# Paired 512-column matmuls in the feed-forwards, roots pair by pair in the first mixture, the difference attention's norm as work in front

## The reference, cut to what matters

```python
# first mixture (gated linear attention), per head of 128 values
o = gla_chunked(q, k, v, log_g)
o = o * rsqrt(mean(square(o), -1) + 1e-5) * head_g
o = from_heads(o) * silu(r)
out = concat([o, memory_attention(qm, mem)]) @ w_out
...
# second block, two layers
h = rms_norm(x, ffn1_norm); x = x + 0.5 * (silu(h @ w_gate) * (h @ w_up)) @ w_down   # 1024 -> 2816 -> 1024
h = rms_norm(x, mix_norm)
o_a = neighborhood_attention(...)        # 4 heads  ("na")
o_b = diff_attention(...)                # 4 heads of two softmaxes, then rms_norm per head  ("df")
o_c = gqa_axial_attention(...)           # 4 heads  ("gq")
o_d = dilated_attention(...)             # 4 heads  ("dl")
x = x + concat([o_a, o_b, o_c, o_d]) @ w_out
h = rms_norm(x, ffn2_norm); x = x + 0.5 * (silu(h @ w_gate) * (h @ w_up)) @ w_down
```

## Time and profile before

| | |
|---|---|
| median of 3 runs | 3088.6 us (3087.66 to 3089.96) |
| the profiled execution's own time | 3092.74 us |
| its span | 3090.5 us |
| busy in the span: PE, DVE, ACT, POOL | 3000.8 us (97%), 2109.8 us (68%), 1628.2 us (53%), 469.1 us (15%) |
| chain that ended last | PE 89%, DVE 6%, ACT 3%, issue 1% |
| mean granted TensorE clock | 0.983 of full speed |
| DMA | 509.47 MB, 165 GB/s |

### The profile page before, as it was taken

The page is one execution under the profiler, slowest core; times in us unless marked ns, Lnnn a source line. Parts: engine busy times, 40 slices in busy tenths (PEclk is TensorE's granted clock), DMA queues, the critical chain, the costliest instruction groups (busy, mean ns, idle before and its releaser), DMA issues.

```text
span 3090.5 us, 56441 instructions
## 1 busy us (share of the span) xinstructions
PE 3000.8 (97%) x21828; PEld 2712.4 (88%) x21828; DVE 2109.8 (68%) x4512; ACT 1628.2 (53%) x3157; POOL 469.1 (15%) x363
## 2 busy tenths in 40 slices
PE   8989999999999989999999999899989999998999
PEld 8789999988887879999998888799868999987898
DVE  4559978799755555997879965655765565566555
ACT  5445544454555555554444455555655555565554
POOL 1212200000022112220000012123101222311122
PEclk9999999999999999999999999999999999999999
DMA  6345554454555335554454555465423556542354
GB/s 216 121 144 182 181 175 161 158 170 164 191 191 177 127 100 174 178 186 163 160 166 163 167 198 191 153 219 185 152 75 132 189 176 214 185 162 76 130 184 157
DMA packets 138363, 509.47 MB, mean 165 GB/s; under 512 B 15329, under 2 KB 15858, under 8 KB 136818
## 3 DMA queue, kind: packets, MB, share of 16 engines
q1 hardware_dynamic: 134352, 489.22, 48.0%
q10 hardware_dynamic: 3746, 16.65, 1.5%
HBM read 504.76 MB, written 1.05 MB: 164 GB/s over the span
## 4 chain that ended last, share of the span: by engine, by line
PE 89%; DVE 6%; ACT 3%; issue 1%; DMA 0%; POOL 0%; ACTq 0%; DVEq 0%
PE ps L475 88%; PE ps L479 1%; ACT WH L1152 1%; DVE WL L1758 1%; ACT BIG L1291 1%; DVE XTl L1830 0%; DVE BIG L1994 0%; DVE BIG L1799 0%; DVE BIG L2500 0%; DVE BIG L1847 0%; DMA BIG<-in_memT 0%; DVE BIG L1989 0%; DVE BIG L2451 0%; DVE H L1924 0%; DVE BIG L1855 0%
## 5 line engine op out<-in xcount | busy, mean ns | idle before, releaser
L1152 ACT ACTIVATE WH<-RAW 128x512 fp32r<-128x512 f32 x1866 | 1158.4, 630 | 1082.1 <-PE ps L475 1068.7
L1758 DVE TENSOR_TENSOR WL<-RAW,WH 128x512 fp32r<-128x512 f32 x1537 | 1102.7, 725 | 710.1 <-ACT WH L1152 698.8
L475 PE MATMUL ps<-XTh,WH 128*128 128x256 f32 x3928 | 1128.4, 287 | 19.8 <-DVE XTl L1807 8.7
L475 PE MATMUL ps<-XTl,WH 128*128 128x256 f32 x3928 | 1118.4, 285 | 0.0
L475 PE MATMUL ps<-XTh,WL 128*128 128x256 f32 x3928 | 1118.0, 285 | 0.0
L2562 POOL TENSOR_TENSOR WL<-RAW,WH 128x512 fp32r<-128x512 f32 x329 | 440.5, 1339 | 2593.6 <-ACT WH L1152 2593.6
L475 PEld LDWEIGHTS ps<-XTh,WH 128*128 128x128 f32 x3928 | 760.2, 194 | 28.6 <-issue 9.8
L475 PEld LDWEIGHTS ps<-XTl,WH 128*128 128x128 f32 x3928 | 760.8, 194 | 2.9
L475 PEld LDWEIGHTS ps<-XTh,WL 128*128 128x128 f32 x3928 | 760.2, 194 | 0.0
L475 PE MATMUL ps<-WH,GH 128*128 128x512 f32 x1056 | 420.2, 398 | 6.5 <-DVE BIG L2435 2.0
L475 PE MATMUL ps<-WH,GL 128*128 128x512 f32 x1056 | 413.7, 392 | 0.0
(11 more groups left out here) (197 smaller groups left out, 2590.7 us busy)
## 6 DMA issues: line engine op xcount, KB each, us to landing
RAW<-in_w SPq DMA_DIRECT2D x933, 512.0 KB, 3.3
BIG<-in_ln ACTq DMA_DIRECT2D x4, 1024.0 KB, 7.8
BIG<-in_sk ACTq DMA_DIRECT2D x2, 1024.0 KB, 5.1
BIG<-in_na_bias ACTq DMA_DIRECT2D x2, 1024.0 KB, 5.0
BIG<-in_qk_gain ACTq DMA_DIRECT2D x2, 960.0 KB, 5.8
BIG<-in_memT ACTq DMA_DIRECT2D x4, 256.0 KB, 7.6
BIG<-in_xT ACTq DMA_DIRECT2D x1, 1024.0 KB, 5.3
H<-in_x ACTq DMA_DIRECT2D x1, 1024.0 KB, 8.1
```

The source lines that it names most:

```text
L475: return self.e.matmul(out, lhsT, rhs, start=start, stop=stop, skip_group_check=loose)
L1152: e.activation(wh, raw, ACT.Copy).then_inc(*c.hi.mark(j))
L1758: e.tensor_tensor(wl, raw, wh.bitcast(F32), ALU.subtract).then_inc(*c.lo_v.mark(j))
```

## The change

1. **Feed-forwards.** `XTh` and `XTl` become two halves of one tensor `XT`, so that each chunk's 512 columns lie side by side. From group 2 on, gate and up have a bank each (6 and 7 for even f, 4 and 5 for odd), and `wide_cols` does, per half of the weights, four matmuls of 512 columns (high weights with both parts of the tokens) and four of 256 (low weights with the high part). The two halves of the bank must then be added: ScalarE copies columns 256 to 512 of both banks (`PARTS`), and VectorE adds them.
2. **The difference attention's norm.** `od` is taken out of `bg`, and is put in `fg` by `attend` as soon as df is complete. `until` waits for `"od"` ahead of chunk 2 of the output product. `until` now prefers `bg`, except for `"od"`.
3. **First mixture.** The decays are multiplied pair by pair; sum, logarithm, exponential, Newton step and gated product are made for each pair of heads (`gla_root`, `gated_heads`) as soon as it is there. The last part of `vr` is evicted with Silu, for which a tiny Silu loads the table beforehand.
4. **Evictions.** `halves(n, done)` on ScalarE waits for `used` and evicts ahead of the last half's other work and split (GLA, SBM, queries of PEER).
5. **First depth product.** `depth` with `first` waits for each bank where it is first written, and does the second block of tokens first.

```diff
@@ Pace
     def until(self, name):
         while name not in self.reached:
-            q = self.fg or self.bg
+            q = self.bg if self.bg and name[1] != "od" else self.fg or self.bg
@@ Chip
+        self.XT = sb("XT", [P, 8, 512], FR)
+        self.XTh, self.XTl = self.XT[:, :, 0:256], self.XT[:, :, 256:512]
+    def ffn_banks(self, f):
+        if f < 2:
+            return self.B[4 + f][:, 0:256], self.B[4 + f][:, 256:512]
+        return (self.B[6], self.B[7]) if f % 2 == 0 else (self.B[4], self.B[5])
@@ Tensor
+    def wide_cols(self, key, ps):
+        c = self.c
+        for half in range(2):
+            j, wh, wl = self.half(key)
+            parts = blocks(4)
+            for a in range(4):
+                self.mm(ps[:, :], wh[:, parts[a]], c.XT[:, half * 4 + a, :], half + a == 0, half * 4 + a == 7, loose=True)
+            for a in range(4):
+                t = self.mm(ps[:, 0:256], wl[:, parts[a]], c.XTh[:, half * 4 + a, :], False, half * 4 + a == 7, loose=True)
+            t.then_inc(*c.used.mark(j))
+            self.pace.tick()
     def depth(self, key, ah, al, first):
-            for blk in range(2):
-                t = self.three(c.B[blk * 2 + half][:, :], ah[:, TB[blk]], al[:, TB[blk]], wh, wl, first, False)
+            for blk in (1, 0) if first else (0, 1):
+                out = c.B[blk * 2 + half]
+                if first:
+                    out = self.bank(blk * 2 + half)
+                t = self.three(out[:, :], ah[:, TB[blk]], al[:, TB[blk]], wh, wl, first, False)
     def inner(self):
-            e.wait_ge(*c.vec.at("ke"))
+            e.wait_ge(*c.vec.at("qe", p))
     def ffn_stage(self, layer, which):
-            ps = self.bank(4 + f % 4)
-            self.cols(("fg", layer, which, f), ps[:, 0:256], stage if f == 0 else None)
-            self.cols(("fu", layer, which, f), ps[:, 256:512])
-            self.empty[4 + f % 4] = c.vec.at(stage, "hid", f)
+            if f < 2:
+                ...
+            else:
+                for b, key in zip((6, 7) if f % 2 == 0 else (4, 5), ("fg", "fu")):
+                    self.wide_cols((key, layer, which, f), self.bank(b))
+                    self.empty[b] = c.vec.at(stage, "hid", f)
     def attend(self, stage, name, k):
+        if name == "df":
+            self.pace.fg.append(od_steps(self.pace, stage))
     def mix_stage(self, layer):
-        pace.bg.insert(2, od_steps())
-                         lambda ch: pace.until((stage, NAMES[ch // 2])))
+                         lambda ch: pace.until((stage, "od" if ch == 2 else NAMES[ch // 2])))
@@ Scalar
-    def halves(self, n):
-        for _ in range(n):
+    def halves(self, n, done=None):
+        for k in range(n):
             self.j += 1
+            if done and k == n - 1:
+                self.e.wait_ge(*self.c.used.at(self.j - 1))
+                done()
             self.pace.tick()
             self.split()
     def states(self):
+            if p:
+                self.gla_root(p - 1)
+            if p == 2:
+                e.activation(t.rs[:, 63:64], c.ONE, ACT.Silu).then_inc(*c.act.mark())
     def gla_stage(self):
-            self.halves(8)
-            e.wait_ge(*c.used.at(self.j - 1))
-            for blk in range(2):
-                e.activation(t.vr[...], c.B[2 * (r % 2) + blk][:, :], ACT.Copy)
+            def done():
+                for blk in range(2):
+                    e.activation(t.vr[...], c.B[2 * (r % 2) + blk][:, :], ACT.Silu if r == 2 else ACT.Copy)
+            self.halves(8, done)
-        e.wait_ge(*c.vec.at("sum", 2))
-        self.rsqrt(t.rs[:, 0:12], ..., "rsum")
-        e.activation(t.vr[:, :, 1024:1536], t.vr[:, :, 1024:1536], ACT.Silu).then_inc(*c.act.mark("silu", 1))
         e.preload_act_table_set(TABLES)
+        self.gla_root(2)
     def hidden(f):   # feed-forward
+            if f >= 2:
+                for k, ps in enumerate(c.ffn_banks(f)):
+                    e.wait_ge(*c.used.at(BASE[stage] + 4 * f + 2 * (f - 2) + 1 + 2 * k))
+                    if f >= 4:
+                        e.wait_ge(*c.vec.at(stage, "hid", f - 2))
+                    e.activation(t.PARTS[:, 2 * r + k, :], ps[:, 256:512], ACT.Copy).then_inc(*c.act.mark(stage, "parts", f, k))
@@ Vector
     def inner(self):
-        e.tensor_tensor(t.qT, t.qT, t.EB, ALU.mult).then_inc(*c.vec.mark())
-        e.tensor_tensor(t.EN, t.EN, t.kT, ALU.mult).then_inc(*c.vec.mark())
+        for p in range(3):
+            e.tensor_tensor(t.qT[:, p], t.qT[:, p], t.EB[:, p], ALU.mult).then_inc(*c.vec.mark())
+            e.tensor_tensor(t.EN[:, p], t.EN[:, p], t.kT[:, p], ALU.mult).then_inc(*c.vec.mark("qe", p))
     def states(self):
+            if p == 2:
+                self.gla_root(0)
+                self.gated_heads(0)
     def hidden(f):   # feed-forward
+            else:
+                e.wait_ge(*c.act.at(stage, "parts", f, 0))
+                e.tensor_tensor(t.GR[:, r, :], gate[:, 0:256], t.PARTS[:, 2 * r, :], ALU.add).then_inc(*c.vec.mark())
+                self.own()
+                e.tensor_tensor(t.GR[:, r, :], t.GR[:, r, :], c.RB, ALU.mult).then_inc(*c.vec.mark(stage, "gr", f))
+                e.wait_ge(*c.act.at(stage, "parts", f, 1))
+                e.tensor_tensor(t.UP[:, r, :], up[:, 0:256], t.PARTS[:, 2 * r + 1, :], ALU.add).then_inc(*c.vec.mark("up", stage, f))
+                up = t.UP[:, r, :]
+                self.own()
```

125 lines of the change are left out of this document (68 added, 57 removed).

## The result

The changed kernel takes 3068.3 us (median of 6 runs, 3063.28 to 3073.09), the one before beside it 3088.1 us (3087.41 to 3089.96): a ratio of 0.9935, interval 0.9922 to 0.9948. A second set of the same kernel gave 3071.2 us (3064.48 to 3072.72) and the same ratio, 0.9935 [0.9921, 0.9949]. It is faster by about 20 us; 30.6 were forecast. The profiled execution took 3072.22 us with a span of 3070.3 and a mean granted clock of 0.987.

A forecast was written before the change was run, and what follows sets the result against it. TensorE's own list was taken to bound PEER and feed-forwards, and waits for other engines the joints and mixtures. Savings of 15.4 + 9.0 + 3.6 + 2.6 = 30.6 us from 3088.6 gave 3058 us, range 3046 to 3073.

The forecast's parts named there:

- the high end: Top of the forecast range, 3073 us: mixture waits only move (3067), plus lower bounds of chain (2.4) and other evictions (2.6).
- The low end: Bottom of the forecast range, 3046 us, said to take the mixtures at their upper bound.
- The pace: Feed-forwards: one matmul fewer per chunk saves 13.3 ns, 360.0 to 346.7 ns; 1280 chunks give 17.0 us less.
- 512-column starts further apart than 0.23 us: Feed-forwards: a trace sign, listed in advance, that would show the prediction wrong.
- the remainder is not per matmul: Feed-forwards: rival that a chunk keeps its 360 ns, giving 0 in place of 17.0 us, 3075 us; chance 0.06.
- The Trainium skill's rule: Feed-forwards: gap of columns over 2.4 GHz plus 2.5 ns; about 3 us saved instead of 17, total 3072 us.
- The tail: End of each feed-forward stage: the longer chain costs 0.4 us per stage, 1.6 us for four.
- The chain of `hidden`: Feed-forwards: chain grows 0.48 us from 3.57, free inside a stage with 1.4 us left.
- Mixtures: Second block's mixtures: 3.9 us wait becomes 2.3, clock returns 2.5, banks 0.4; 4.5 us each, 9.0 for both.
- Stage 0: First mixture: 1.9 us wait, 1.5 clock and 0.5 eviction saved, 0.3 new waiting; 3.6 us less.
- The decays pair by pair I cost at nothing: First mixture: pairwise decays cost nothing, since TensorE is in a half while VectorE makes them.
- Other evictions: PEER copies one split earlier save 1.1 us, the stick-breaking wait for the last bank 1.5; together 2.6 us.

The follow-up runs named there:

- last_narrow: product_later with the last block (21) of each feed-forward in the old narrow form, in one bank; 3064.2 us, ratio 0.9921.
- product_later: silu_later plus, on VectorE, pair 0's root and product behind the sum of pair 2, and pairs 1 and 2's behind the preceding low copies; 3063.9 us, ratio 0.9921.
- silu_later: The changed kernel with the first mixture's small table-loading Silu moved on ScalarE behind the high copy of pair 3; 3064.4 us, ratio 0.9918.
- root0_early: product_later with pair 0's root and product back ahead of the sum of pair 2; 3066.8 us, ratio 0.9928.
- undo_stage0: The changed kernel with the first mixture's pairwise roots, products, decays and merged Silu put back as before, early evictions kept; 3074.8 us, ratio 0.9950.
- both_fixes: root0_early and last_narrow together; 3066.6 us, ratio 0.9926.
- undo_ffn: The changed kernel with its feed-forwards put back: one bank per block, three 256-column matmuls a chunk; 3075.1 us, ratio 0.9957.
- undo_norm: The changed kernel with the difference attention's norm back in the background queue and the old order of `until`; 3077.2 us, ratio 0.9963.
- undo_evict: The changed kernel with evictions behind their half's split again and four banks waited for at once; 3069.3 us, ratio 0.9934.
- alternate: The changed kernel with wide and narrow feed-forward matmuls in turn, one of each, instead of four and four; 3071.4 us, ratio 0.9940.
- long_bursts: The changed kernel with eight wide then eight narrow feed-forward matmuls, both halves of the weights held; 3106.4 us, ratio 1.0050.

## Why the prediction was right, and where not

The time lies in the range and on the forecast side, at 20 of the forecast 30.6 us. That it lies in the range is in part luck: the high end was made of mixtures that give nothing and of lower bounds of the chain and the evictions, none of which came, while the two things that cost most, the pace and stage 0, had no such room. The low end is added up wrongly: the mixtures at their upper bound give 3058 - 8.8 = 3049 us, and 3046 only with the best bounds of the other terms as well. By its steps:

**The pace.** "A chunk costs ... 226.7 + 120.0 = 346.7 ns" is the step that was mis-sized. Mixed streams don't run at the pace of pure ones: 232.5 ns for a wide matmul behind narrow ones. A chunk is 350.6 ns over the burst, a group is 0.147 us shorter and not 0.213, and 80 groups give 11.8 us for 17.0. Of the 0.066 us a group that are missing, three bursts of wide ones cost 0.07 and the depth product behind the last narrow burst 0.02 (2.77 us for 2.75), and the narrow ones give 0.03 back. "512-column starts further apart than 0.23 us" was among the prediction's own signs of being wrong, and came. The number stood in the trace of before, 0.93 us for the first four of a depth product; the earlier trace rows took the 512 columns from a stream of their own width. The rival "the remainder is not per matmul" had named the place ("grow where a wide one follows"), at 0.06 and at the full price; it came at a third of it. The Trainium skill's rule in "TensorE: Matmul & The Clock Gate", section "Back-to-back issue gap", would have had a chunk at an estimated 325.0 ns; no stream in these traces comes near that, pure (226.7 and 120.0 ns a matmul) or mixed. Its total of 3072 us lies close to the measured one, but only since stage 0 missed its term by 6 us and the mixtures passed theirs by 4.

**The ends of a stage.** The tail was put at 0.4 us and is 0.48 in stage 4 (5.64 us from the start of the loop's last depth product to the first addition, 5.15 before; the 5.75 and 5.27 in the expectation of last_narrow are each 0.1 too long, and their difference is right); last_narrow shows its cause, the copies and sums of the last block. What I missed is the start: the spacing of the first two depth products is 9.43 us against 9.09, which with 0.147 less due is 0.49 us lost. Part of it is the longer wait for GpSimd's low part, 0.46 for 0.30, the rest a gap of 0.2 us ahead of 2021.5 and a burst behind it that takes 1.03 us. With 11.8 - 4 x 0.97 = 7.9 us the four stages should gain 2.0 each, which stage 4 does, and the others at like clock (193.48 to 191.41, 191.92 to 189.90, 193.28 to 191.17). The profiled pair shows 6.7 since stage 7's joint had a fall of the clock after and none before, 1.5 us.

**The chain of `hidden`** came as worked out (4.07 us), and free inside a stage, as said.

**Mixtures.** The mechanism was right in each step: maxima ahead of the norm, the wait of 3.9 gone, new waits of 0.47 and 1.29 where 0.6 and 1.7 were forecast, plus 0.39 that I hadn't. The gain was larger, 12.7 for 9.0 (12.8 in the second trace). TensorE's idle time gave 4.6 us of it, for 4.0 forecast (1.6 + 0.4, twice). The term mis-sized is the clock: I gave each mixture 2.5 us back, 5.0 in all, and some 8 went with it here, differently in each trace.

**Stage 0** is where the prediction was wrong in sign: -3.6 forecast, +2.5 measured from split 57. The failed step is "the copy of its turned values stands behind a table load (1.28 us) and two splits; I expect 0.3 us of waiting". I looked at ScalarE's queue and not at VectorE's. The copy on ScalarE was done at 138.56, ahead of TensorE's wait. On VectorE pair 1's root and product stand ahead of the low copy of pair 0, which TensorE needs first. The waits that were to go did shrink (1.90 to 0.56 at the first depth product, 1.1 to 0.5 ahead of the rows of v). product_later, which only reorders VectorE's and ScalarE's work, turns +2.5 into -1.1, and silu_later and root0_early show that neither the table load nor pair 0's place did it: pair 1's work ahead of the low copy is the cause. The 3.6 of the forecast was not reached by any order that I tried. "The decays pair by pair I cost at nothing" held for this pair of kernels, which both have no wait there, but undo_stage0 shows what it hides: with the evictions early and the decays undone TensorE waits 1.89 us, and the clock falls.

**Other evictions.** 3.8 us for 2.6, of which the waits that were named give 2.5: 2.1 to 0.9 and 1.5 to 0.2 us. The remainder is in the stages' lengths, where I didn't trace it further.

Best measured: product_later, silu_later and last_narrow, at 3063.9 to 3064.4 us with one ratio, 0.992; by the stages at like clock both_fixes is the shortest and last_narrow 0.1 us behind it, both some 5 us ahead of the changed kernel. The medians alone can't tell this from falls of the clock.

## What to carry to other kernels

When work is moved early, list for each engine that it runs on what now stands behind it, and who needs that first; a reordering on one queue is only safe when the other queues of the same step have been read too. Take the pace of a mixed instruction stream from a mixed stream: look for a place in the trace where the one kind follows the other, however short (here four matmuls), and where there is none, keep a margin on the sum. Where the clock's state differs between executions, compare stages at like clock and not medians: an edit worth 1 to 4 us drowns in falls worth 1.5 us each. And where an edit is undone whole, read the whole stage for its effect and not only the place that was in mind.

## What the runs showed of the hardware

- A 512-column matmul started 226 to 227 ns after the last in a stream of its own width, and 232.5 ns on the mean of the four behind a burst of 256-column ones, in the kernel before as well (0.93 us for the first four of a depth product); in turn one by one, the pair took 353 ns. What causes the extra 6 ns stays open.
- The same program, with the same idle time ahead of it, was granted the full clock at a joint of stages in one execution and not in the next, at 1.5 us each.
- VectorE and GpSimd slow each other down, depending on what VectorE reads. In the changed kernel's trace, of 121 low parts `WL` (two inputs in SBUF, 128x512) that VectorE began while a GpSimd operation ran, 117 took longer than their usual 0.69 us, 1.36 at the median and up to 1.80; 12 products of 128x1 took 0.80 to 1.11 us instead of 0.16. Those with an input in PSUM (ten of 128x128 at 0.29, four of 128x256 at 0.41 us), reductions, maxima and reciprocals kept their time. L1829 at 138.26 is such a case (1.25 us instead of 0.16), the GpSimd operation beside it took 1.85 instead of 1.29, and L1829 takes 1.24 to 1.26 us in all eight traces that have this order of work (the two of the changed kernel, undo_ffn, undo_norm, undo_evict, silu_later, alternate, long_bursts).
